# Latent attention: the rotation moved beside the up projection, only the values turned in its own stage, semaphores cleared once at the end

## The reference, cut to what matters

```
q = (rmsnorm(cq, q_norm_g) @ w_uq).reshape(Bsz, S, H, MLA_NOPE + MLA_ROPE)
q_nope, q_pe = jnp.split(q, [MLA_NOPE], axis=-1)
q_pe = apply_rope(q_pe, cos[:, :, None, :], sin[:, :, None, :])
kv = (rmsnorm(ckv, kv_norm_g) @ w_ukv).reshape(Bsz, S, H, MLA_NOPE + MLA_V)
k_nope, v = jnp.split(kv, [MLA_NOPE], axis=-1)
k_pe = apply_rope(k_rope, cos, sin)
sc = q_nope . k_nope + q_pe . k_pe          # causal, times scale
o = softmax(sc) @ v
```

## Time and profile before

| | |
|---|---|
| median of 3 runs | 4723.36 us (4720.06 to 4728.51) |
| the profiled execution, its span | 4711.8 us, 4710.0 us |
| PE, PEld busy | 4485.6 us (95%), 3823.1 us (81%) |
| DVE, ACT, POOL busy | 3131.1 us (66%), 1715.3 us (36%), 951.8 us (20%) |
| mean granted TensorE clock | 0.983 of 2.4 GHz |
| `mla_up`, layers 0 and 1 | from 2421.8 and from 3801.5 us |
| turn stage, layers 0 and 1 | from 2483.5 and from 3862.5 us |
| attention | from 2497.1 and from 3876.1 us |

### The profile page before, as it was taken

The page is one execution under the profiler, slowest core; times in us unless marked ns, Lnnn a source line. Parts: engine busy times, 40 slices in busy tenths (PEclk is TensorE's granted clock), DMA queues, the critical chain, the costliest instruction groups (busy, mean ns, idle before and its releaser), DMA issues. The chain is left out here.

```text
span 4710.0 us, 60762 instructions
## 1 busy us (share of the span) xinstructions
PE 4485.6 (95%) x23048; PEld 3823.1 (81%) x23048; DVE 3131.1 (66%) x5390; ACT 1715.3 (36%) x2861; POOL 951.8 (20%) x918
## 2 busy tenths in 40 slices
PE   9889899999999999988999999999988999999999
PEld 7428689999999999877787778888877777878887
DVE  6586757899978888876555565533775655665443
ACT  4414433334433333433333343422423434353332
POOL 4661005564532333022000011000022000020000
PEclk9899999999999999989999999999999999999999
DMA  3013135798989999300221213233201221213332
GB/s 117 27 36 94 50 94 170 255 304 279 307 299 353 341 339 336 121 27 22 87 75 55 77 51 115 90 99 97 87 5 50 86 75 40 90 50 108 100 97 81
DMA packets 236465, 610.74 MB, mean 130 GB/s; under 512 B 23312, under 2 KB 108560, under 8 KB 235024
## 3 DMA queue, kind: packets, MB, share of 16 engines
q1 hardware_dynamic: 199312, 472.62, 31.4%
q0 software_dynamic: 36864, 134.23, 7.9%
HBM read 557.22 MB, written 49.55 MB: 129 GB/s over the span
## 5 line engine op out<-in xcount | busy, mean ns | idle before, releaser
L553 DVE TENSOR_TENSOR weight_low<-ring,weight_high 128x1024 fp32r<-128x1024 f32 (+2 forms) x648 | 760.1, 1173 | 952.6 <-PE banks L106 895.7
L541 ACT CAST weight_high<-ring 128x1024 fp32r<-128x1024 f32 (+2 forms) x728 | 730.1, 1005 | 535.4 <-PE banks L106 522.7
L104 PE MATMUL banks<-x_high,weight_high 128*128 128x512 f32 x1856 | 760.8, 410 | 30.0 <-DVE weight_low L553 16.9
L105 PE MATMUL banks<-x_low,weight_high 128*128 128x512 f32 x1856 | 729.4, 393 | 0.0
L106 PE MATMUL banks<-x_high,weight_low 128*128 128x512 f32 x1856 | 728.7, 393 | 0.0
L553 POOL TENSOR_TENSOR weight_low<-ring,weight_high 128x1024 fp32r<-128x1024 f32 (+1 forms) x22 | 50.4, 2295 | 2037.7 <-PE banks L106 1876.9
L104 PEld LDWEIGHTS banks<-x_high,weight_high 128*128 128x128 f32 x1856 | 352.0, 190 | 122.8 <-issue 26.7
L105 PEld LDWEIGHTS banks<-x_low,weight_high 128*128 128x128 f32 x1856 | 352.5, 190 | 82.1 <-issue 10.6
L106 PEld LDWEIGHTS banks<-x_high,weight_low 128*128 128x128 f32 x1856 | 352.2, 190 | 75.3
L104 PE MATMUL banks<-xn_high,weight_high 128*128 128x384 f32 x1024 | 353.8, 345 | 16.5 <-POOL weight_low L562 15.8
L105 PE MATMUL banks<-xn_low,weight_high 128*128 128x384 f32 x1024 | 343.3, 335 | 0.0
(11 more groups left out here) (678 smaller groups left out, 9691.2 us busy)
## 6 DMA issues: line engine op xcount, KB each, us to landing
ring<-in_peer_u SPq DMA_DIRECT2D x128, 512.0 KB, 4.5
ring<-in_peer_v SPq DMA_DIRECT2D x128, 512.0 KB, 5.4
ring<-in_w_up SPq DMA_DIRECT2D x64, 512.0 KB, 3.5
ring<-in_w_down SPq DMA_DIRECT2D x64, 512.0 KB, 3.5
ring<-in_w_gate SPq DMA_DIRECT2D x48, 512.0 KB, 3.6
acts<-dot_act SPq DMA_DIRECT2D x124, 192.0 KB, 4.1
activations<-acts SPq DMA_DIRECT2D x124, 192.0 KB, 5.5
ring<-in_w_gdn_in SPq DMA_DIRECT2D x34, 512.0 KB, 3.6
```

The source lines that it names most:

```text
L104: nc.tensor.matmul(out, w_high, x_high, start=start, stop=False)
L105: nc.tensor.matmul(out, w_high, x_low, start=False, stop=False)
L541: self.nc.scalar.copy(self.wH[:, g % HIGHS, 0:kc * P], self.ring[:, g % SLOTS, 0:kc * P]).then_inc(self.high_made, 1)
L553: ops.tensor_tensor(self.wL[:, g % LOWS, 0:kc * P], self.ring[:, g % SLOTS, 0:kc * P], self.wH[:, g % HIGHS, 0:kc * P].bitcast(F32), ALU.s ...
```

## The change

Four things. (1) `mla_up` now begins with the four tiles of the rotated query parts and then does the other eight of `mla_uq`. A new object `Rotation`, given to `linears` in `norms`, puts the five swap matmuls behind tiles 3, 5, 7, 9 and 11 into banks 4 to 6; DVE multiplies the bank by the sines in place and, one tile later, adds it; the multiplication by the cosines goes to POOL. (2) The turn stage holds only the transposes; their copies alternate between ACT and DVE, and POOL writes the two key copies. (3) ACT's `act_end` comes at job step 33, ahead of its last two stores. (4) The barriers behind `Weights.clear`, `Rows.clear` and `Fetched.clear` are gone, and `Fetched`'s twelve semaphores live until the end of the program and are cleared there.

```diff
@@ Weights.clear, Rows.clear, Fetched.clear: in each
-        self.nc.all_engine_barrier()
@@ attention, ACT's list, for j in range(len(jobs) + MIXED_FROM + TT + 1)
                 if 0 <= h < heads and part == parts:
                     store(h)
+                if beside and j == len(jobs) + 1:
+                    beside.act_end(act)
                 if 0 < h <= heads and parts == TT and part == 0:
                     store(h - 1)
-            if beside:
-                beside.act_end(act)
@@ the new class Rotation
+    def pe_at(self, pe, i):
+        n, half = divmod(i - self.at, 2)
+        if half or not 0 <= n < len(self.turning):
+            return
+        if n:
+            pe.wait_ge(self.source.done[-1], n)
+        if n >= 3:
+            pe.wait_ge(self.rotated, n - 2)
+        self.nc.tensor.matmul(self.bank(n), self.swap, self.turning[n], start=True, stop=True).then_inc(self.swapped, 1)
+    def dve_at(self, dve, i):
+        n, half = divmod(i - self.at - 1, 2)
...
+        if half == 0:
+            dve.wait_ge(self.swapped, n + 1)
+            self.nc.vector.tensor_tensor(self.bank(n), self.bank(n), self.sinT, ALU.mult).then_inc(self.sines, 1)
+        else:
+            dve.wait_ge(self.sines, n + 1)
+            dve.wait_ge(self.cosines, n + 1)
+            self.nc.vector.tensor_tensor(x, x, self.bank(n), ALU.add).then_inc(self.rotated, 1)
+    def pool(self, pool):
+        for n, x in enumerate(self.turning):
+            pool.wait_ge(self.swapped, n + 1)
+            self.nc.gpsimd.tensor_tensor(x, x, self.cosT, ALU.mult).then_inc(self.cosines, 1)
@@ latent_attention, the turn stage
             @block.scalar
             def _(act):
-                for n, c in enumerate(order):
+                for n in range(0, 8, 2):
...
+            @block.gpsimd
+            def _(pool):
+                pool.wait_ge(turned, 1)
+                nc.gpsimd.memset(odd_key[0:64, :], 0.0)
+                nc.gpsimd.tensor_copy(odd_key[second, :], latents(6)[second, :]).then_inc(key_copied, 1)
+                pool.wait_ge(key_copied, 1)
+                nc.gpsimd.memset(latents(6)[second, :], 0.0)
             @block.vector
             def _(dve):
...
+                for n in range(1, 8, 2):
+                    dve.wait_ge(turned, n + 1)
+                    nc.vector.tensor_copy(vals[...], tiles4(banks[n % 4])).then_inc(by_dve, 1)
```

More of the change, by code:

```diff
@@ L2072, with __init__, place @@
 class Fetched:
-    def __init__(self, nc, held, at):
+    def __init__(self, nc, held):
+        self.a_in = [held.enter_context(nc.semaphore(f"act{u}_loaded")) for u in range(HELD)]
+        self.g_in = [held.enter_context(nc.semaphore(f"gate{u}_loaded")) for u in range(HELD)]
+    def place(self, nc, at):
         self.A = nc.alloc_sbuf_tensor_at("activations", [P, HELD, DENSE], F32, offset=at)
         self.G = nc.alloc_sbuf_tensor_at("gates_in", [P, HELD, STORED_GATES], F32, offset=at + 4 * HELD * DENSE)
-        self.a_in = [held.enter_context(nc.semaphore(f"act{u}_loaded")) for u in range(HELD)]
-        self.g_in = [held.enter_context(nc.semaphore(f"gate{u}_loaded")) for u in range(HELD)]
     def load(self, eng, dram, c):
@@ L2088, in clear @@
             nc.gpsimd.sem_clear(sem)
-        nc.all_engine_barrier()
 def combine(nc, dram, weights, fetched, hT, banks, rope, ahead, scratch, pairs, ident, room, acts, act_pair, rows_at, sum_at):
@@ L2341, in second_block @@
         acc = [scratch[:, s, :] for s in range(SLOTS)]
-        with ExitStack() as combining:
-            fetched = Fetched(nc, combining, fetched_at)
-            combine(nc, dram, weights, fetched, hT, banks, RopeTables(nc, dram, const, cosT[:], sinT[:], vecs, scratch),
-                    Ahead(weights, dram["w_gdn_in"], 0), scratch, pairs, ident, room, acts, act_pair, rows_at, parts_at)
-            fetched.clear(nc)
+        fetched.place(nc, fetched_at)
+        combine(nc, dram, weights, fetched, hT, banks, RopeTables(nc, dram, const, cosT[:], sinT[:], vecs, scratch),
+                Ahead(weights, dram["w_gdn_in"], 0), scratch, pairs, ident, room, acts, act_pair, rows_at, parts_at)
         def col(name, k=0):
@@ L2780, in _, with __init__, take, bank @@
                     nc.gpsimd.tensor_tensor(CE[:, h % 4, :], CE[:, h % 4, :], xp[:, 10 + h // 8, 0:T], ALU.mult).then_inc(c_scaled, 1)
+class Rotation:
+    NAMES = "swapped sines_made cosines_made rotated"
+    def __init__(self, nc, key, queries, swap, cosT, sinT, banks, at, source):
+        self.nc, self.turning, self.swap, self.cosT, self.sinT, self.banks = nc, [key, *queries], swap, cosT, sinT, banks
+        self.at, self.source = at, source
+    def take(self, sems):
+        self.swapped, self.sines, self.cosines, self.rotated = sems
+    def bank(self, n):
+        return self.banks[4 + n % 3]
+    def pe_at(self, pe, i):
[7 more added lines that the diff above has]
+        self.nc.tensor.matmul(self.bank(n), self.swap, self.turning[n], start=True, stop=True).then_inc(self.swapped, 1)
+    def act_at(self, act, i):
+        pass
+    def dve_at(self, dve, i):
+        n, half = divmod(i - self.at - 1, 2)
+        if not 0 <= n < len(self.turning):
+            return
+        x = self.turning[n]
+        if half == 0:
[9 more added lines that the diff above has]
+            self.nc.gpsimd.tensor_tensor(x, x, self.cosT, ALU.mult).then_inc(self.cosines, 1)
 def latent_attention(nc, dram, layer, qT, latents, yT, xn, col, cst, ones, weights, rstd, banks, ident, scratch, tools, spare, cosT, sinT):
@@ L2810, in latent_attention @@
                 Linear("mla_uk", dram["w_mla_uk"], layer * 8, 8, 2, ckv, scaled(k_of, rstd_kv), fed=late),
                 Linear("mla_uv", dram["w_mla_uv"], layer * 8, 8, 2, ckv, scaled(v_of, rstd_kv))],
-                weights, banks, fold=fold, fold_late=late, ahead=Ahead(weights, dram["w_gate"], layer * 24 + 8))
+                weights, banks, fold=fold, fold_late=late, norms=[rotation], ahead=Ahead(weights, dram["w_gate"], layer * 24 + 8))
         vals = sb("mla_v", [P, TT, D])
         pr = sb("mla_probs", [P, 3, T])
-        first_sines, odd_key = pr[:, 2, :], spare[:, 1, :]
@@ L2817, in latent_attention @@
-        with stage(nc, "mla_swapped mla_turned mla_copied mla_rotated dve_step split_step") as (
-                block, swapped, turned, copied, rotated_one, dve_step, split_step):
-            turning = [latents(6)] + [rotated[:, f, :] for f in range(4)]
-            order = (7, *range(7))
+        odd_key = spare[:, 1, :]
+        with stage(nc, "mla_turned copied_by_act copied_by_dve key_copied") as (block, turned, by_act, by_dve, key_copied):
+            order, second = (7, *range(7)), slice(64, P)
@@ L2822, in _ @@
             @block.tensor
             def _(pe):
-                for n, x in enumerate(turning):
-                    if n >= 3:
-                        pe.wait_ge(rotated_one, n - 2)
-                    nc.tensor.matmul(banks[4 + n % 3], cst("swap"), x, start=True, stop=True).then_inc(swapped, 1)
                 for n, c in enumerate(order):
                     if n >= 4:
-                        pe.wait_ge(copied, n - 3)
+                        pe.wait_ge(by_dve if n % 2 else by_act, (n - 4) // 2 + 1)
@@ L3268, in program @@
         pairs = Rows(nc, held)
+        fetched = Fetched(nc, held)
         tools = (roots, eps, ident[:], columns, ones[:])
```

32 lines of the change are left out of this document (9 added, 23 removed).

## The result

| | before | after |
|---|---|---|
| median of the timed executions, beside each other | 4721.91 us of 5 (4720.06 to 4728.51) | 4698.57 us of 5 (4695.25 to 4701.48) |
| the profiled execution, its span | 4711.8, 4710.0 us | 4697.76, 4695.7 us |
| mean granted TensorE clock | 0.983 | 0.984 |

The ratio is 0.9947, with an interval of 0.9935 to 0.9959: faster, by 23.3 us of median. The kernel after was timed again later, beside the experiments `z0_after` and `z1_both`: 4699.34 us of 6 (4697.32 to 4701.82), ratio 0.9955 [0.9941, 0.9969]. The forecast was 4704.3.

The account below looks back on a forecast made before the run. PE bounds the up projection; DVE's rotations end the turn stage. Per layer 3.75 - 8.8 - 1.45 - 2.2 = -8.7, twice -17.4; with -2.0 and +0.3, -19.1 us: 4723.4 to 4704.3 us, range 4694 to 4717.

Parts of the forecast that it names:

- The four places: PE-bound up projection, turn stage ended by DVE's rotations, attention's end with the gate's splits, seam between expert layer and second block.
- +3.75: Up projection, per layer: four swaps on PE's path, 3.48 us, plus 0.27 of the first; DVE and POOL add nothing.
- one or two meetings of under 1 us: Up projection: POOL's products hold up DVE's splits this often, at tiles with 0.6 to 1.4 us to spare.
- Rival C: Up projection: DVE becomes the bound of tiles 4 to 13, 14.9 us more a layer, 4734 us in all; chance 0.04.
- rival B: PE waits for splits 2 to 4 us a layer, or POOL's key copies end the turn stage; 4708 to 4713; shared chance 0.20.
- The turn stage: Per layer, from PE's start to the attention's first matmul: 4.8 us instead of 13.63, so -8.8 (-7.7 to -9.0).
- the clock behind it: Attention's first job, per layer: full instead of half clock after a shorter PE standstill, 2.05 instead of 3.52 us, -1.45.
- The attention's end: Per layer: the gate's last splits run earlier, -2.2 us; PE's wait goes from 4.61 to 2.4, half clock behind it.
- rival A: Attention's end: the clock stays full behind the 2.4 us wait, 2 x 1.5 us more gain, 4701.3; chance 0.15.
- The clearing: Behind combine: -2.0 us once, from 2.94 to 0.88 between POOL's end and PE's start; bounds -1.0 and -2.1.
- the 11.6 us: Profiled execution of before stood this far below the median of the runs; the forecast applied its gain to the median, 4723.4.
- Rival D: Attention's first jobs wait for ACT or DVE, so its gaps are worth less: 4709.4 us; shared chance 0.20.

Follow-up runs that it names:

- z0_after: The changed kernel once more, unchanged, timed against the kernel before: 4699.34 us of 6, ratio 0.9955 [0.9941, 0.9969].
- z1_both: Changed kernel with the cosine products back on DVE and two small matmuls behind the attention's last mixing: 4696.02 us of 6, ratio 0.9948 against the kernel before.
- y1: Changed kernel with the five products by the cosines on DVE in place of POOL: 4697.6 us, one profiled execution.
- y3: Changed kernel with the all-engine barrier behind combine put back, the twelve clears still at the program's end: 4698.75 us, one profiled execution.
- y4: Changed kernel with all eight value copies of the turn stage on ACT, none on DVE: 4702.56 us, one profiled execution.
- x2: Kernel before with only the gate's last ACT split moved ahead: 4713.2 us of 11, ratio 0.9981 [0.9972, 0.9990].
- x0: The kernel before, unchanged, timed against itself: 4720.23 us of 11, ratio 0.9992 [0.9983, 1.0001].
- x1: Kernel before with only the clearing moved (three barriers gone, twelve clears at the end): 4718.3 us of 11, ratio 0.9994 [0.9984, 1.0004].
- x3: Kernel before with only the rotation beside the up projection and the turn stage with values alone: 4705.21 us of 5, ratio 0.9965 [0.9952, 0.9979].

## Why the prediction was right, and where it was off

**What bounds the kernel.** The four places were the right ones. PE stayed the bound of the up projection, and DVE's rotation was what ended the turn stage: with it gone the stage took 4.74 us against 4.8.

**The up projection: +4.0, not +3.75.** Four swaps at 0.87 on the path was right (0.86 measured). The first was to hide in PE's 0.60 wait but for 0.27, and that was misread. By starts, which the text itself names as the measure, tile 4's first matmul came 0.99 us after the one ahead of it (at 2433.50) where 0.23 is usual, and the next 0.10 later than usual: the wait cost 0.87, and the swap hides in it whole. The wait of 0.56 at tile 5 costs 0.82 by the same count (2438.41 to 2439.36, then 0.33 for 0.23). In the kernel before there was one more small delay ahead of tile 8, 0.26, which is gone. So 4 x 0.86 + 0.82 - 0.26 = 4.0. The place that the text named for POOL's hold was the splits; it fell on the pair L614, one instruction earlier, when POOL's first product started 0.48 us into it. The pair took 1.03 longer, and the wait went on to tile 5. y1 shows it: without POOL's product the pair is 1.41 long and the stage +3.66 (some short delays of DVE's, 0.4 us in all, stand at later tiles there). That is the "one or two meetings of under 1 us", but at a tile where nothing was to spare. The Trainium skill, "SBUF — State Buffer", section on the two separate sides, says that whichever of the two starts first holds the shared ports for its whole instruction while the other waits. The trace fits it in both orders: behind POOL's product the pair's second instruction took 1.78 instead of 0.75, and where DVE's split had begun first, at 2450.40, POOL's product took 1.69 instead of 1.29 to 1.41, and DVE's split 0.68. Added up, though, the hold came to 0.35 us a layer, and not to five products. DVE's work at tile 5 (reciprocal and first sum) cost nothing, as forecast. Rival C did not come, and of rival B only these 0.35 us.

**The turn stage and the clock behind it.** The stage ended 3.65 + 1.1 us after its start, with DVE's copy last. POOL's two memsets and copy took 0.52, 0.61 and 0.52 us, half of the value taken, and were covered as said. The first job took 1.91 instead of 2.05: -1.6 where -1.45 was forecast. The value was read from job 4, of which I took off the 0.67 of wait; by starts (0.94 us where 0.11 is usual) the wait cost 0.83, and 2.72 - 0.83 = 1.89.

**The attention's end.** -2.2 and a wait of 2.39 instead of 2.4, as forecast. The choice between forecast and rival A, whether the clock comes back at its lower level, is one that this wait does not settle. Of eleven attention ends with a wait of 2.39 in six profiled executions (after, y1, y3, y4, z0 with both layers, x2 with layer 0) three kept the full clock (x2 once, y3 twice) and eight fell, at a price of 1.6 us each. At 4.6 all fell (before, x0, x1, x3), at 1.94 one of two, at 1.76 none of two. At 2.59 the one there was (x2, layer 1) fell. The kernel after's two profiles, after and z0, show the forecast's side four times out of four; that the choice came right was luck, since y3 and x2 show the other side behind the same wait.

**The clearing: -1.1, not -2.0.** This is the term that was most off. I compared with the seam behind `mla_tail`, 0.88 us from POOL's end to PE's start, and took all above it for the clearing. The two seams are not alike. y3 and x1 take the one behind combine apart: barrier 0.33, twelve clears 0.78, and 1.83 are left between POOL's end and PE. Of these, 1.55 are POOL's drain, which ends that long after its last instruction at this place in all twelve profiles, where behind `mla_tail` it is 0.07. The 0.88 there was DVE's time: its drain ends 0.60 after POOL's last instruction, and PE starts 0.27 after that. What POOL's drain waits for was not tried. The estimates of 0.075 a clear and some 0.1 to 0.3 for a barrier, which the text made for the end of the program, were near (0.065 and 0.33 here) and would have given 1.0 to 1.2 had I used them at this place too: the bound of -1.0 was the better value. The end of the program cost 0.2 against 0.3.

**The sum and what was put on it.** -19.1 forecast, -18.3 in the stages; errors of both signs are in it (+0.5 for the up projection, -0.2 for the turn stage and -0.3 for the first jobs, both layers each, +0.9 for the clearing, -0.1 at the end). The total was met less well than its terms: 4704.3 against 4698.57. The step that failed is the last one, the 11.6 us by which the profiled execution of before stood below the median, put on the forecast unchanged. The profiled execution after took 4697.76, 5.1 above the 4692.7 worked out for it, and stood 0.8 below its median. Of the 5.1, 0.8 are the terms' and the rest lies in stages that nobody changed: the first block was 4.0 longer in that execution, to combine's end. The 55 timed executions of before in this study, x0's with them, lie between 4708.3 and 4729.0, with a mean granted clock from 0.984 down to 0.979 (on record for 50); the 11 of after between 4695.3 and 4701.8. The profiled one of x1 shows where 10.7 of such a surplus lay: in the first block. There the profiled execution of before was the quickest of all twelve, 3.5 us under their average, so that much of its distance was luck. Part of the 5 us that the median gains beyond the stages can be placed. The profiled execution of before was lucky in its attention too: over the six attentions of before, x0 and x1 the stage took 115.77 to 116.70, 116.20 on average, and the `mla_tail` behind it 45.43, against 115.89 and 45.22 there. With the idle time of 5.61 gone, the ten attentions of after, y1, y3, y4 and z0 took 112.06 to 112.10. That is 0.5 a layer, 1.0 in all. At the end of the attention the clock was kept at two ends of those ten, 1.6 us each; if that is the kernel after's own rate, 0.6 more are placed (an estimate; its own two profiles show none of four). The rest stays open. Each series alone hardly tells it from noise: 19.3 us lies inside z0's interval (14.6 to 27.9) and at the edge of the first one (19.4 to 30.7), and x0 stood 3.1 from the same kernel. All executions taken together, with medians of 4722.1 and 4698.9 and again 23.2 apart, speak for a real difference. The kernel after also scatters less, and no experiment tells why. x2 is narrower than x0 and x1 too (8 us against 18 and 19, of 11 executions each), x3 as well (9, but of 5).

**Rival D**, that gaps are worth less than they look, is out: both of the attention's gaps were worth their full size: the first job fell to 1.91 us, and the stage by 1.6 + 2.2.

## What to carry to other kernels

A chain on one engine that ends a stage can be moved beside a stage bound by another engine: five rotations cost 4.0 us there instead of 8.9, and behind the shorter standstill PE ran the next stage's start at its full clock. Price a wait by the starts around it, not by the idle time printed: 0.60 printed was 0.87 here. When POOL gets a product with both operands in SBUF, look at which DVE instruction it starts beside, not only at the free time of both; here giving it back to DVE was cheaper. And before a profiled execution's distance from the median is carried over to a forecast, see where the median of the same kernel lies in its own scatter: it was the largest error here, larger than that of any term. Before two seams are compared, see which engine ends last in each.

## What was not expected of the hardware

- The same wait of PE (2.39 us) was followed by the lower clock eight times and by the full one three times, in the same stage of nearly the same program; 1.94 went both ways as well, and ahead of the turn stage the clock fell behind 1.87 (x2) and held behind 2.72 (x1).
- The drop needn't be there when the work starts again. In z1_both the first matmul takes 0.47 in both layers, and then they part: 0.43 and 0.63 against 0.39 and 0.39. In the kernel after, layer 0, the first one already takes 0.67.
- POOL's memset and copy of 64x512 floats took 0.52 and 0.61 us, while its product of 128x512 took 1.29 to 1.69, twice DVE's 0.68.
- A pair of DVE instructions with both operands in SBUF went from 1.41 to 2.44 us beside one POOL product of 1.41: nearly the whole product was added to it.
- A barrier of all five engines cost 0.33 us between two stages, and the clearing of a semaphore on POOL 0.065.
- POOL's drain in the barrier behind combine ended 1.55 us after POOL's last instruction, in all twelve profiles; behind `mla_tail` 0.07.
